# 128 bytes of padding ahead of the long-lived tiles of a two-block transformer kernel

## What is computed

```python
# block 1
h = rmsnorm(x); x = x + hybrid_mixer(h, w_in, ...)          # gated delta rule + chunk gating, @ w_out
x = x + memory_cross_attention(rmsnorm(x), m, w_q, w_k, w_v, w_o)
x = x + square(relu(rmsnorm(x) @ w1)) @ w2                   # 1024 -> 4096 -> 1024
# block 2
proj = rmsnorm_2(x) @ w_in_2 + b_in_2
y_conv = (cb * causal_dwconv_2(cc * cx, conv_mix_w)) @ w_conv_out
y_attn = sliding_window_attention(q, k, v, sinks) @ w_attn_out + b
x = x + (sigmoid(g_conv) * y_conv + sigmoid(g_attn) * y_attn) @ w_mix_out
up, gate = split(rmsnorm_2(x) @ w_ffn_up)                    # 2 x 2816
x = x + (silu(conv(up)) * gate) @ w_ffn_down
out = rmsnorm_2(x)
```

## The kernel before

| tile | first byte | place in a 512-byte line |
|---|---|---|
| w_raw | 16512 | 128 |
| w_hi, w_lo | 32896, 49280 | 128, 128 |
| a_hi, a_lo | 65664, 82048 | 128, 128 |
| matrices | 99648 | 320 |
| temp0 to temp4 | 116032 to 124352 | 320 to 448 |
| gain12 (the last one ahead of the change) | 126432 | 480 |
| x_first, xs | 126464 | 0 |
| b_hi, b_lo | 142848, 159232 | 0, 0 |
| qkv, inv, inv_t, level_b, xa_q | 142848 to 198144 | 0 |
| ws, small | 210464, 214560 | 32, 32 |

## Time and profile before

### The profile page before, as it was taken

One profiled execution on the slowest core, in us unless ns is written; L12 is line 12 of the kernel. 1 busy time (PEld: TensorE's weight loads), 2 busy tenths in 40 slices (PEclk: granted clock), 3 DMA queues, 4 the chain that ended last, 5 costly groups with the idle time before them and its releaser, 6 DMA issues.

```text
span 1686.9 us, 19688 instructions
## 1 busy us (share of the span) xinstructions
PE 1633.9 (97%) x7828; PEld 1342.9 (80%) x7828; DVE 894.1 (53%) x1239; ACT 596.8 (35%) x866; POOL 172.2 (10%) x138
## 2 busy tenths in 40 slices
PE   6899999989999999999999999999999999999997
PEld 5689897978778888888887777777788888888885
DVE  4676754644435434343656566544555564564454
ACT  4543423433334423142443333354333332332231
POOL 4141221202002000000034000000002000000000
PEclk9899999999999999999999999999999999999998
DMA  6111111343113323223222222221232233223221
GB/s 250 38 38 51 51 38 51 113 162 100 51 38 113 100 88 100 95 93 107 88 90 85 75 88 75 76 88 63 77 120 94 87 103 100 89 94 108 92 75 50
DMA packets 42843, 147.32 MB, mean 87 GB/s; under 512 B 4800, under 2 KB 4928, under 8 KB 42624
## 3 DMA queue, kind: packets, MB, share of 16 engines
q1 hardware_dynamic: 40608, 140.68, 25.3%
q10 hardware_dynamic: 1584, 2.88, 0.5%
q0 software_dynamic: 560, 2.50, 0.4%
HBM read 143.94 MB, written 2.10 MB: 87 GB/s over the span
## 4 chain that ended last, share of the span: by engine, by line
PE 66%; issue 23%; DVE 6%; ACT 3%; POOL 1%; DMA 1%; ACTq 0%; SPq 0%; POOLq 0%; DVEq 0%
PE bank L1122 19%; PE bank L1124 19%; PE bank L1123 19%; DVE temp L1629 1%; PE bank L1252 1%; PE bank L1234 1%; PE bank L1315 1%; PE bank L1332 1%; DMA x_first<-x_in 1%; PE bank L1257 1%; PE bank L1372 1%; DVE w_lo L1636 1%; PE bank L1081 1%; PE bank L1352 1%; PE bank L1088 1%
## 5 line engine op out<-in xcount | busy, mean ns | idle before, releaser
L1122 PE MATMUL bank<-a_hi,w_hi 128*128 128x512 f32 (+1 forms) x1368 | 535.2, 391 | 13.2 <-ACT a_hi L1399 10.7
L1123 PE MATMUL bank<-a_lo,w_hi 128*128 128x512 f32 (+1 forms) x1368 | 524.0, 383 | 0.0
L1124 PE MATMUL bank<-a_hi,w_lo 128*128 128x512 f32 (+1 forms) x1368 | 523.7, 383 | 0.0
L1636 DVE TENSOR_TENSOR w_lo<-w_raw,w_hi 128x1024 fp32r<-128x1024 f32 (+2 forms) x267 | 344.8, 1292 | 195.3 <-ACT w_hi L1389 194.9
L1389 ACT ACTIVATE w_hi<-w_raw 128x1024 fp32r<-128x1024 f32 (+2 forms) x267 | 274.5, 1030 | 206.1 <-PE bank L1124 206.1
L1122 PEld LDWEIGHTS bank<-a_hi,w_hi 128*128 128x128 f32 x1368 | 260.4, 190 | 68.0 <-issue 15.0
L1124 PEld LDWEIGHTS bank<-a_hi,w_lo 128*128 128x128 f32 x1368 | 260.3, 190 | 50.5
L1123 PEld LDWEIGHTS bank<-a_lo,w_hi 128*128 128x128 f32 x1368 | 260.5, 190 | 47.8 <-issue 1.2
L1122 PE MATMUL bank<-b_hi,w_hi 128*128 128x512 f32 x720 | 285.4, 396 | 0.2 <-ACT b_hi L1519 0.2
L1124 PE MATMUL bank<-b_hi,w_lo 128*128 128x512 f32 x720 | 284.4, 395 | 0.0
L1123 PE MATMUL bank<-b_lo,w_hi 128*128 128x512 f32 x720 | 284.2, 395 | 0.0
(11 more groups left out here) (268 smaller groups left out, 1199.5 us busy)
## 6 DMA issues: line engine op xcount, KB each, us to landing
w_raw<-weights_in SPq DMA_DIRECT2D x251, 512.0 KB, 3.3
w_raw<-weights_in SPq DMA_DIRECT2D x8, 384.0 KB, 3.1
xs<-x_in ACTq DMA_DIRECT2D x8, 256.0 KB, 5.8
w_raw<-weights_in SPq DMA_DIRECT2D x8, 256.0 KB, 2.6
out<-xs SPq DMA_DIRECT2D x8, 256.0 KB, 2.1
x_first<-x_in SPq DMA_DIRECT2D x6, 256.0 KB, 12.2
mem_x<-mem_in POOLq DMA_DIRECT2D x1, 1024.0 KB, 12.4
matrices<-matrices_in POOLq DMA_DIRECT2D x1, 640.0 KB, 8.8
```

Of the source, the lines that this page charges most:

```text
L1122: pe.matmul(to, w_hi[:, slot, at], hi, start=k == k0, stop=False)
L1123: pe.matmul(to, w_hi[:, slot, at], lo, start=False, stop=False)
L1124: t = pe.matmul(to, w_lo[:, slot, at], hi, start=False, stop=k == k1 - 1)
L1636: dve.tensor_tensor(w_lo[:, n % SLOTS, 0:size], raw[:, n % SLOTS, 0:size], w_hi[:, n % SLOTS, 0:size].bitcast(F32), ALU.subtract).then_inc ...
```

## The change

One tile of 32 float32, 128 bytes per partition, is declared behind `gain12` and the PSUM banks and ahead of `x_first`. Nothing reads or writes it. It belongs to the base stack, so it stays for the whole kernel, and every tile that is declared behind it begins 128 bytes further on. Tiles ahead of it stay where they were. No instruction is added, removed or moved, and no wait.

```diff
@@ -731,6 +731,8 @@
         gain12 = sbuf("gain12", [P, KT])
         banks = [base.enter_context(nc.psum_tensor(f"bank{i}", [P, S], F32)) for i in range(8)]
 
+
+        sbuf("line_pad", [P, 32])
         x_first = ExitStack()
         x0 = sbuf("x_first", [P, KT, S], stack=x_first)
         x_first.close()
```

## The result

| | before | after |
|---|---|---|
| median | 1685.43 us (4 runs) | 1675.76 us (4 runs) |
| lowest, highest | 1684.43, 1687.89 | 1675.05, 1676.83 |
| ratio, 95% interval | | 0.9941 [0.9924, 0.9958] |
| span of the profiled execution | 1686.9 | 1673.3 |
| PE busy | 1633.9 | 1619.5 |

The changed kernel is 0.6% faster, 9.7 us by the medians. The forecast was 1672.7 us in a range of 1667.4 to 1681.

What follows compares the result with a forecast made beforehand. TensorE's matmul pace was taken as the bound, busy 97% of the span. Term (1) saved 13.1 us and the others counted as nothing, so 1685.75 - 13.1 = 1672.7 us, range 1667.4 to 1681.

Steps and rivals of the forecast that it cites:

- The candidate: Tiles b begin at place 0 of a 512-byte line, tiles a and split weights at 128; this costs b 6.5 ns a matmul.
- the three things that could matter: For the pace on tiles b: b's own place, its place relative to the weight block loaded under it, or b's height.
- Term (1): Products streaming tiles b (ffn_w2, down2, conv_out2, attn_out2, w_out, xa_wo, mix2) take the pace of tiles a: 13.1 us saved.
- Term (2): After faster b units the next weights, splits and evacuation might come late; loss put at nothing.
- Terms (3) and (4): Plain float32 matmuls, and VectorE and ScalarE on moved tiles: 0 each; bounds 1.7 us either way and 7 ns an instruction.
- Term (5): Loads into moved tiles such as x_first: taken as 0, bound 1.9 us either way.
- the half: Rival "Half of it": on tiles b only the 0.24 us step goes, saving 9.3 us, 1676.5 us; chance 0.10.
- Nothing changes: Rival: b's height or a cause outside its place sets the pace; b stays at 233.3 ns, 1685.75 us; chance 0.14.
- Slower: Rival: b isn't helped and some 1000 plain float32 matmuls streaming moved tiles lose 6.5 us, 1692.3 us; chance 0.04.

Runs made afterwards that it cites:

- b alone moved: Kernel before with 128 bytes of padding right ahead of b_hi; tiles b and what follows move, x_first, xs and delta rule tiles stay: 1675.91 us, ratio 0.9938.

## Why the prediction was right

**The bound and the way to read it.** That TensorE's pace is the bound, and that it is in the starts and not in the durations, has held: with the seams equal, the time went down, and no wait of PE took its place. (One reading was off: the clock stands at nine tenths or more in 38 of the 40 slices, not 39; nothing hangs on it.)

**The candidate.** The step that ruled out all but the lowest and the uppermost part of the address was right, and the experiment with moved weights has separated the two: the height plays no part. Of the three things that could matter it was the place relative to the weights. The argument that all multiples of 512 are harmless has held for the long stretches; that 256 is harmless too could not be seen in a kernel whose tiles differ by 128.

**Term (1), 13.1 us.** Measured from the begin of w_out to the last large product: 13.15 us. w_out fell from 44.69 to 43.65 us from seam to seam, 1.04 where 1.08 was forecast; each full ffn_w2 stretch fell by 1.27 us, forecast 1.25.

**Term (2), nothing late.** Right: the weights kept up, and ScalarE's and VectorE's waits for TensorE shrank by 10 us each, somewhat less than the saving of 13.

**Terms (3) and (4), nothing.** Right: 276 ns and 693 ns as before. For TensorE it is the starts again that count, and `inv` with `level_b` and `matrices` with `small` both go at 112 ns from start to start, before and after. **Term (5), nothing:** right too, the two loads of `x_first` from ScalarE's queue still land in 4.5 us at the new place.

**What the sum lacked.** The forecast of 1672.7 is met by the executions with few steps of the lower clock: 1672.82 us with 384 bytes of padding, 1672.12 with b alone moved, 1673.65 for the third trace of the change. The median of the change is 3 us above it, a quarter of term (1), and nearer to the 1676.5 us of the half than to the forecast: by the time alone the two can't be told apart, only by the starts. The prediction took the scatter of the runs, 1.7 us, as one that is the same on both sides. It comes in the main of steps of 1.6 to 1.7 us each, and the changed kernel has had more of them; another 0.95 us, between the traces without steps, goes behind the last product. The trace of before held two steps behind 300 us, too short to be seen in the 40 slices of the earlier trace rows, and the prediction gave them no term and no range of their own.

**The rivals.** "Nothing changes" by height is refuted by the moved weights. "Half of it", that only the longer of the two steps goes, is refuted by the even steps after: both have gone to 226.7. "Slower" has not come about; the plain float32 groups take what they took. The rule of the Trainium skill, page "TensorE: Matmul & The Clock Gate", section "Step-by-step: what each phase is for", that loading the next weights takes no bandwidth from the running matmul, doesn't account for what was measured: the distance between the two tiles alone moves the pace from 226.7 to 233.3 ns. That the two reads hold each other up is the likely reading, but no run shows the reads themselves. Nor does the count by lines of 16 bytes of the Trainium skill, page "SBUF — State Buffer", section "Door 1: The DMA port swizzle (why `[64,N]` ≈ `[32,N]`)", foretell it: all the distances tried are multiples of 16, and four of the six are slow.

## What to carry to other kernels

Where two groups of matmuls of the same shape and type go at different paces, subtract the starts at their seams and compare where their streamed tiles and their weights begin. Here, in long stretches, float32r products of 512 columns cost 2.9% more whenever the two places differed by 32, 64 or 128 bytes, and nothing when they differed by 0 or 256; those of 256 columns cost nothing either way, and in groups of twelve among short matmuls agreeing places brought less than half as much. The padding took 128 bytes of each partition and no time. A gain of some 10 us in a kernel that waits now and then must be judged by several runs with their granted clock, since a few steps at the lower level are worth as much as a third of it.

## What the runs showed of the hardware

The place of the streamed tile relative to the weights sets the pace: 6.6 ns more on each float32r matmul of 512 columns, one size for three different distances, with a pattern that returns after 256 bytes. With `w_lo` alone out of place two of three matmuls pay it, the one under which it is loaded and the one that uses it. Float32r matmuls of 256 columns don't pay it (120 and 119 ns). Nor do plain float32 matmuls of 128 columns: from start to start `inv` with `level_b` and `matrices` with `small` take 112 ns before and after, and the transposes with `matrices` and `qkv` take 109 ns before, where the two are 64 bytes apart modulo 256, and 109 ns with 64 bytes of padding, where they agree.

The granted clock falls to its lower level for 3.4 us at a few places behind partly idle stretches, in some executions and not in others; one such step costs 1.6 to 1.7 us here.
